# Values one head later and scores ahead of a sum in an attention, and experts chosen by one maximum and one replacement

## The chip, the core and the metric

The kernel runs on one core of a Trainium2 chip. A core has five engines that run their own instruction streams and meet only at semaphores: TensorE (PE in the profile, with its weight loads as PEld), VectorE (DVE), ScalarE (ACT), GpSimd (POOL) and SyncE (SP), which here only issues transfers. The metric is the device time of one execution, in microseconds (us); lower is better.

## The reference

The program is two transformer blocks on 256 tokens of width 1024, in float32. The first block has two mixers side by side: an eight-head causal attention with compressed queries and keys (MLA), and an RWKV-7 recurrence. Then comes a mixture of 32 experts, of which each token takes 4. The second "block" is two layers of dense FFN and mixers. What the change touches is the attention of the first block and the choice of experts:

```python
def one_block(args):                       # causal_attention, 8 heads, Q_BLOCK = 128
    qb, bi = args
    scores = jnp.einsum('bqhd,bkhd->bhqk', qb, k, preferred_element_type=jnp.float32) * scale
    ...
    probs = jax.nn.softmax(scores, axis=-1).astype(v.dtype)
    return jnp.einsum('bhqk,bkhd->bqhd', probs, v)

logits = (ht @ router_w + router_b).astype(jnp.float32)     # moe_ffn, 256 tokens x 32 experts
top_val, top_idx = lax.top_k(logits, TOP_K)                 # TOP_K = 4
gates = jax.nn.softmax(top_val, axis=-1)
...
counts = jnp.bincount(e_flat, length=N_EXPERTS)
```

In between, `mod = silu(c) @ ada_w + ada_b` gives six vectors that shift, scale and gate the blocks; the kernel computes them in three thirds.

## The kernel before

The program is a row of stages, each a block of five streams written by hand, with a barrier at its end; nothing reorders instructions inside a stream. `Steps.step` lets an engine signal a semaphore and wait for it itself; `Steps.tell` only signals. Tensors lie transposed, channels on the 128 partitions and tokens along the row.

Weights of 1 MB each come through `ring` (12 slots of 8 KB per partition), and later also `ring_odd`. SP issues a load as soon as the semaphore `used` says that TensorE has finished with what was in the slot.

The **attention stage** (`c3`, from line 634 on). TensorE first makes the second third of `mod` (`sum_ada(pe, 1, ...)`), then queries and keys head by head, their rotated partners (`partner`, with DVE's `rotate`) and the values' inputs `v_nat`. Then `sum_ada(pe, 2, bank[5])` makes the last third: 32 products with 8 MB of weights. ACT copies the sum to `mod_rows`, TensorE turns it, DVE adds the bias. Only then `att_pe`, `att_dve` and `att_act` run, which `attention(n, scale)` has built. In them one head goes through:
- TensorE `scores(h)` into bank h % 2 (L522), two heads ahead;
- DVE `soften(h)`: mask (L558), row maximum (L560), its negative (L562);
- ACT `exps(h)`: exponential and its sum (L597);
- DVE `divide(h)`: reciprocal (L567) and scaling (L570);
- TensorE `turn(h)`: three 128x128 transposes (L530);
- ACT: the copy `turned` (L606);
- TensorE `values(h)`: two products (L538, L539); for each second head DVE's `take` copies the result (L575).

The **choice of experts** is the end of stage `c7` (from line 1395 on). After a layer norm ACT makes `hT` in eight pieces (L1486), TensorE multiplies each by the router's weights (L1452) into four groups, ACT copies `groups` (L1488), TensorE adds them (L1457), and DVE adds the bias: `logits`, 128 tokens x 2 tiles x 32 experts. Four rounds on DVE find the largest, mark the first place where it stands (`hit`, with the helper numbers `rev`), add the mark to `chosen` and lower it in `work`. `chosen_ready` lets TensorE count, with triangular and full matrices of ones in float32 (L1463 to L1467), each token's rank within its expert. DVE makes `rank`, and `passes`, the number of times that the loop over experts has to run (64 slots each). ACT meanwhile copies `h_nat`, scales `xT` for the residual (L1494, L1498) and makes the exponential of the shifted logits for the `gates` (L1496). Then the stage ends, each engine reads `passes`, and the expert stage begins (`pick`, L1783; gather; the products with the experts' weights, whose first loads into freed slots SP issues while the first expert is being computed).

## Time and profile before

| | |
|---|---|
| median of three runs | 2384.93 us |
| the three runs | 2393.33, 2380.46, 2384.93 us |
| the profiled execution | 2385.3 us |
| its span, first to last instruction | 2383.5 us |
| mean granted TensorE clock | 0.965 |
| busy: PE, PEld, DVE, ACT | 2204.9, 1595.3, 1098.5, 701.9 us |
| DMA | 626.63 MB, mean 263 GB/s |

### The profile page before, as it was taken

What the parts mean: (1) busy time and instruction counts of PE and PEld (TensorE: products, weight loads), DVE (VectorE), ACT (ScalarE), POOL (GpSimd) and SP (SyncE); (2) the same over time, 40 slices, a digit from 0 to 9 for tenths busy, and PEclk for the clock granted to TensorE, in tenths of its full rate; (3) what the DMA queues carried; (4) which work ended last, traced back from release to release, by engine and by line L of the source; (5) the groups of instructions that cost most, each with busy time, mean ns of one, the idle gap of its engine ahead of it and who ended that gap; (6) DMA issues with size and microseconds to landing.
All of it is one profiled execution on the core that took longest, in us unless ns stands there. A gap on an engine that the chain in (4) does not pass through costs nothing. (4 is left out here: it accounts for less than half of the span.)

```text
span 2383.5 us, 37791 instructions
## 1 busy us (share of the span) xinstructions
PE 2204.9 (93%) x15730; PEld 1595.3 (67%) x15730; DVE 1098.5 (46%) x1701; ACT 701.9 (29%) x889; POOL 16.9 (1%) x16
## 2 busy tenths in 40 slices
PE   6978869999999999999997999999999999999998
PEld 4637733443333333333336999989999999989997
DVE  4567331221111111111116666777556656677664
ACT  3353231111111111111114334545334334445332
POOL 0002000000000000000000000000000000000000
PEclk9988989999999999999998999999999999999999
DMA  9640279999999999999985655334565555433651
GB/s 390 257 175 3 98 299 424 424 425 425 425 425 425 425 426 425 426 425 425 414 351 170 202 186 173 119 105 136 195 194 171 184 188 166 142 106 125 208 180 53
DMA packets 233056, 626.63 MB, mean 263 GB/s; under 512 B 13144, under 2 KB 149880, under 8 KB 197112
## 3 DMA queue, kind: packets, MB, share of 16 engines
q1 hardware_dynamic: 229736, 622.06, 68.4%
q10 hardware_dynamic: 3216, 3.06, 0.4%
q8 instruction: 80, 1.31, 0.2%
q14 instruction: 24, 0.20, 0.0%
HBM read 624.03 MB, written 1.05 MB: 262 GB/s over the span
## 5 line engine op out<-in xcount | busy, mean ns | idle before, releaser
L1929 DVE TENSOR_TENSOR w_low<-ring,w_high 128x2048 fp32r<-128x2048 f32 x168 | 383.9, 2290 | 266.6 <-ACT w_high L1924 266.6
L1924 ACT ACTIVATE w_high<-ring 128x2048 fp32r<-128x2048 f32 x168 | 320.1, 1910 | 274.2 <-PE bank L2163 140.8
L1682 PE MATMUL bank<-ring,ut 128*64 128x512 f32 x1024 | 252.7, 646 | 43.2 <-DMA ring<-in_exp_w_dram 42.8
L1654 PE MATMUL bank<-ring_odd,xt 128*64 128x512 f32 x1024 | 225.0, 597 | 0.0
L1654 PE MATMUL bank<-ring,xt 128*64 128x512 f32 x1024 | 223.3, 594 | 0.3 <-ACT xt L1736 0.3
L1682 PEld LDWEIGHTS bank<-ring,ut 128*64 128x64 f32 x1024 | 74.2, 146 | 205.9 <-issue 134.5
L2178 PE MATMUL bank<-h_high,w_high 128*128 128x256 f32 x1408 | 187.4, 282 | 6.5 <-ACT h_high L2069 3.6
L2178 PE MATMUL bank<-h_high,w_low 128*128 128x256 f32 x1408 | 186.6, 281 | 1.4 <-DVE w_low L1929 1.4
L2178 PE MATMUL bank<-h_low,w_high 128*128 128x256 f32 x1408 | 186.5, 281 | 1.3 <-DVE h_low L2108 1.3
L2178 PEld LDWEIGHTS bank<-h_high,w_high 128*128 128x128 f32 x1408 | 176.0, 189 | 7.6 <-ACT h_high L2069 4.3
L1740 ACT ACTIVATE sg<-glu 128x512 f32<-128x512 f32 x32 | 20.2, 631 | 543.0 <-DVE glu L1803 543.0
L2178 PEld LDWEIGHTS bank<-h_high,w_low 128*128 128x128 f32 x1408 | 175.8, 189 | 1.7 <-DVE w_low L1929 1.7
L2178 PEld LDWEIGHTS bank<-h_low,w_high 128*128 128x128 f32 x1408 | 175.8, 189 | 1.5 <-DVE h_low L2108 1.5
L1819 DVE SCALAR_TENSOR_TENSOR xT<-bank,mod,xT 128x256 f32<-128x256 f32 x128 | 55.6, 480 | 247.4 <-PE bank L1696 247.4
L1654 PEld LDWEIGHTS bank<-ring_odd,xt 128*64 128x64 f32 x1024 | 72.5, 138 | 144.3 <-issue 144.3
L1654 PEld LDWEIGHTS bank<-ring,xt 128*64 128x64 f32 x1024 | 72.3, 137 | 143.2 <-issue 143.2
L1802 DVE TENSOR_SCALAR lin<-bank 128x256 f32<-128x256 f32 x64 | 26.7, 418 | 257.2 <-PE bank L1654 257.2
L1795 DVE TENSOR_SCALAR choose<-base 128x128 fp32r<-128x128 f32 x32 | 9.1, 287 | 244.0 <-PE bank L1682 244.0
L1753 ACT ACTIVATE y<-bank 64x512 f32<-64x512 f32 x64 | 37.9, 592 | 270.3 <-PE bank L1682 269.5
L2163 PE MATMUL bank<-u_low,w_high 128*128 128x256 f32 x704 | 92.0, 279 | 0.0
L2163 PE MATMUL bank<-u_high,w_high 128*128 128x256 f32 x704 | 91.9, 279 | 0.0
L2163 PE MATMUL bank<-u_high,w_low 128*128 128x256 f32 x704 | 91.9, 279 | 0.0
(542 smaller groups left out, 2834.1 us busy)
## 6 DMA issues: line engine op xcount, KB each, us to landing
ring<-in_exp_w_dram SPq DMA_DIRECT2D x256, 1024.0 KB, 22.0
ring_odd<-in_exp_w_dram SPq DMA_DIRECT2D x128, 1024.0 KB, 21.0
ring<-in_ffn_w_gate_dram SPq DMA_DIRECT2D x44, 1024.0 KB, 5.4
ring<-in_ffn_w_up_dram SPq DMA_DIRECT2D x44, 1024.0 KB, 5.4
ring<-in_ffn_w_down_dram SPq DMA_DIRECT2D x44, 1024.0 KB, 5.0
ring<-in_w_in_dram SPq DMA_DIRECT2D x36, 1024.0 KB, 5.4
ring<-in_ada_w_dram SPq DMA_DIRECT2D x24, 1024.0 KB, 12.5
ring<-in_w_out_dram SPq DMA_DIRECT2D x8, 1024.0 KB, 5.2
```

The lines of the kernel that those rows point to most:

```text
L1654: ins = nc.tensor.matmul(bank[b][at:at + SLOTS, :], xt[:, c, SLOTS * side:SLOTS * side + SLOTS], (ring, ring_odd)[side][:, c, 512 * q:512 ...
L1682: ins = nc.tensor.matmul(bank[2 + dh][64 * dh:64 * dh + 64, :], ut[:, r % 4, 64 * (r // 4):64 * (r // 4) + 64], w[:, x, 512 * dh:512 * dh ...
L1740: nc.scalar.activation(sg[:, :], glu[:, :], ACT.Sigmoid, scale=SW_ALPHA).then_inc(sem("sg_ready"), 1)
L1753: nc.scalar.activation(y[64 * side:64 * side + 64, 512 * dh:512 * dh + 512], bank[2 + dh][64 * dh:64 * dh + 64, :], ACT.Copy).then_inc(sem ...
L1795: nc.vector.tensor_scalar(choose[:, side, :], const("half_of"), const("expert_of")[:, bass.ds(e, 1)], None, ALU.mult).then_inc(sem("chosen ...
L1802: nc.vector.tensor_scalar(lin[:, 256 * b:256 * b + 256], pairs[:, :, 1], LIMIT, -LIMIT, ALU.min, ALU.max)
L1819: ins = nc.vector.scalar_tensor_tensor(xT[:, m, :], bank[6 + n % 2][:, T * j:T * j + T], mod[:, 40 + m:41 + m], xT[:, m, :], ALU.mult, ALU ...
L1924: nc.scalar.activation(w_bufs[0][u % BUFS], ring2[:, u % RING2, :], ACT.Copy).then_inc(high2, 1)
L1929: nc.vector.tensor_tensor(w_bufs[1][u % BUFS], ring2[:, u % RING2, :], w_bufs[0][u % BUFS].bitcast(F32), ALU.subtract).then_inc(low2, 1)
L2163: ins = nc.tensor.matmul(sums(m // 2)[:, T * (m % 2):T * (m % 2) + T], w[:, at:at + P], v[:, T * x:T * x + T], start=(g == 0 and k == 0 an ...
L2178: ins = nc.tensor.matmul(b[:, T * x:T * x + T], w[:, at:at + P], h[:, c, :], start=(k == 0 and x == 0 and c == 0), stop=(k == 2 and c == D ...
```

## The change

In the attention:
- `values(h - 1)` stands ahead of `turn(h)`, behind `scores(h + 2)`; the last `values` comes after the loop.
- The functions take callbacks. `queries_ready(h)` waits only for the rotation of head h's pair. `scores(0)` and `scores(1)` are issued first, then `before_turns` (`sum_ada(pe, 2, ...)`), and `after_second` turns the sum behind `turn(1)`. On ACT the copy of the sum comes behind `exps(1)`, on DVE the bias behind the first `take`.
- The second attention of the kernel, of another block, has its own code and is not touched.

In the choice of experts:
- `hT`: five pieces on ACT, three on DVE (`H_ON_ACT = 5`).
- `nc.vector.max` gives the eight largest logits of each token, one instruction for each tile of 128 tokens; the fifth to eighth are overwritten with `ABSENT` (-3.0e38); `match_replace` copies the logits and puts `TAKEN` (-3.3e38) where one of the remaining four values stands; `chosen` is where copy and logits differ. Four columns that hold `ABSENT` stand behind the 32 logits, to match the four overwritten values.
- `chosen`, `before_r` and `ones_r` are F32R, so each rank product is one MATMUL instead of two; ACT makes the two copies.
- Three comparisons for `passes` become one, against `limits`; the gates come last on DVE.

```diff
...
-            def tensor(pe, S, lhs, rhs, v):
+            def tensor(pe, S, lhs, rhs, v, queries_ready, before_turns, after_second):
...
                 def scores(h):
+                    queries_ready(h)
                     if h >= 2:
...
                 scores(1)
+                before_turns()
...
                         scores(h + 2)
+                    if h:
+                        values(h - 1)
                     turn(h)
-                    values(h)
-            def vector(dve, st, S, mask, dst):
+                    if h == 1:
+                        after_second()
+                values(n - 1)
+            def vector(dve, st, S, mask, dst, after_third):
...
                         take(h // 2 - 1)
+                    if h == 2:
+                        after_third()
                 take(n // 2 - 1)
-            def scalar(act, st, S):
+            def scalar(act, st, S, after_two):
...
                 exps(1)
+                after_two()
...
                 pe.wait_ge(sem("k_taken"), HEADS)
-                sum_ada(pe, 2, bank[5])
-                pe.wait_ge(sem("v_taken"), 1)
-                pe.wait_ge(sem("mod_rows_ready"), 2)
...
-                pe.wait_ge(sem("rotated"), PAIRS_Q)
                 pe.wait_ge(sem("k_spread"), 1)
+                def last_third():
+                    sum_ada(pe, 2, bank[5])
+                    pe.wait_ge(sem("partner_taken"), 1 + PAIRS_Q)
+                    pe.wait_ge(sem("v_taken"), TT)
+                def turn_last_third():
+                    pe.wait_ge(sem("mod_rows_ready"), 2)
+                    for k in range(4):
+                        ins = nc.tensor.transpose(bank[6][:, P * k:P * k + P], mod_rows[:, P * k:P * k + P], ident)
+                    ins.then_inc(sem("mod_turned"), 1)
                 att_pe(pe, S,
...
                        lambda h, keys: k_all[:, h, 0:keys],
-                       lambda h, a: v_nat[:, a, VDIM * h:VDIM * h + VDIM])
+                       lambda h, a: v_nat[:, a, VDIM * h:VDIM * h + VDIM],
+                       lambda h: pe.wait_ge(sem("rotated"), h // 2 + 1),
+                       last_third, turn_last_third)
...
                 nc.scalar.activation(ps[:, 13, :], ps[:, 13, :], ACT.Sigmoid)
-                act.wait_ge(used, UNIT[("ada2", ADA_THIRD - 1)] + 1)
-                act.wait_ge(sem("mod_turned"), 1)
-                st.tell(nc.scalar.activation(mod_rows[:, :], bank[5][:, :], ACT.Copy), "mod_rows_ready")
-                att_act(act, st, S)
+                def last_third():
+                    act.wait_ge(used, UNIT[("ada2", ADA_THIRD - 1)] + 1)
+                    act.wait_ge(sem("mod_turned"), 1)
+                    st.tell(nc.scalar.activation(mod_rows[:, :], bank[5][:, :], ACT.Copy), "mod_rows_ready")
+                att_act(act, st, S, last_third)
...
                 rotate(PAIRS_Q - 1)
-                dve.wait_ge(sem("mod_turned"), 2)
...
-                att_dve(dve, st, S, const("causal3"), lambda pair: hT[:, pair, :])
+                def last_third():
+                    dve.wait_ge(sem("mod_turned"), 2)
+                    dst, bias = mod_third(2)
+                    st.step(nc.vector.tensor_tensor(dst, turned_columns(bank[6][:, :]), bias, ALU.add), "mod_taken")
+                    st.step(nc.vector.tensor_scalar(mod[:, 32:48], mod[:, 32:48], 1.0, None, ALU.add))
+                att_dve(dve, st, S, const("causal3"), lambda pair: hT[:, pair, :], last_third)
...
+            logits = sb("logits", [P, TT, E + 8 - TOPK], where=c7)
...
+            chosen = sb("chosen", [P, TT, E], F32R, where=c7)
+            chosen_f = chosen[:, :, :].bitcast(F32)
+            top = sb("top", [P, TT, 8], where=c7)
...
+            before_r = sb("before_r", [P, P], F32R, where=c7)
+            ones_r = sb("ones_r", [P, P], F32R, where=c7)
...
                 for c in range(DC):
-                    pe.wait_ge(sem("h_ready"), c + 1)
+                    if c < H_ON_ACT:
+                        pe.wait_ge(sem("h_ready"), c + 1)
+                    else:
+                        pe.wait_ge(sem("h_ready_dve"), c - H_ON_ACT + 1)
                     j = c % 4
...
+                pe.wait_ge(sem("rank_parts"), 1)
                 pe.wait_ge(sem("chosen_ready"), 1)
-                nc.tensor.matmul(bank[5][:, 0:E], const("before"), chosen[:, 0, :], start=True, stop=True)
...
+                nc.tensor.matmul(bank[5][:, 0:E], before_r[:, :], chosen[:, 0, :], start=True, stop=True)
+                nc.tensor.matmul(bank[5][:, E:2 * E], before_r[:, :], chosen[:, 1, :], start=True, stop=False)
+                nc.tensor.matmul(bank[5][:, E:2 * E], ones_r[:, :], chosen[:, 0, :], start=False, stop=True)
...
+                nc.tensor.matmul(bank[5][:, 2 * E:3 * E], ones_r[:, :], chosen[:, 1, :], start=False, stop=True).then_inc(sem("ranks_ready"), 1)
...
                     nc.scalar.activation(xT[:, 4 * j:4 * j + 4, :], xT[:, 4 * j:4 * j + 4, :], ACT.Copy, scale=ALPHA).then_inc(sem("x_scaled"), 1)
+                nc.scalar.activation(before_r[:, :], const("before"), ACT.Copy)
+                nc.scalar.activation(ones_r[:, :], ones, ACT.Copy).then_inc(sem("rank_parts"), 1)
                 act.wait_ge(sem("b_loaded"), 128)
...
                 act.wait_ge(sem("h_gain_ready"), 1)
-                for c in range(DC):
+                for c in range(H_ON_ACT):
                     act.wait_ge(sem("scaled"), c // 2 + 1)
...
-                rev = const("rev").unsqueeze(1).to_broadcast([P, TT, E])
+                for c in range(H_ON_ACT, DC):
+                    dve.wait_ge(sem("scaled"), c // 2 + 1)
+                    st.tell(nc.vector.tensor_scalar(hT[:, c, :], xT[:, c, :], h_gain[:, 0, c:c + 1], h_gain[:, 1, c:c + 1],
+                                                    ALU.mult, ALU.add), "h_ready_dve")
+                for j in range(3):
+                    nc.vector.memset(limits[:, j:j + 1], SLOTS * (j + 1) + 0.5)
+                st.step(nc.vector.memset(logits[:, :, E:], ABSENT))
                 wide = lambda ap: ap.to_broadcast([P, TT, E])
+                scores = logits[:, :, 0:E]
                 dve.wait_ge(sem("logits_ready"), 1)
                 dve.wait_ge(sem("router_loaded"), 32)
-                st.step(nc.vector.tensor_tensor(logits[:, :, :], bank[7][:, 0:TT * E].rearrange("p (a e) -> p a e", a=TT),
+                st.step(nc.vector.tensor_tensor(scores, bank[7][:, 0:TT * E].rearrange("p (a e) -> p a e", a=TT),
                                                 b_r[:, :].unsqueeze(1).to_broadcast([P, TT, E]), ALU.add))
-                nc.vector.memset(chosen[:, :, :], 0.0)
-                st.step(nc.vector.tensor_copy(work[:, :, :], logits[:, :, :]))
-                for k in range(TOPK):
-                    st.step(nc.vector.tensor_reduce(top[:, :, k], work[:, :, :], AX_X, ALU.max))
...
-                st.step(nc.vector.tensor_tensor(work[:, :, :], logits[:, :, :], wide(top[:, :, 0:1]), ALU.subtract), "shifted_logits")
-                st.tell(nc.vector.tensor_copy(hit[:, 0, 0:1], top[:, 0, 0:1]), "chosen_ready")
-                dve.wait_ge(sem("exp_ready"), 1)
...
+                for a in range(TT):
+                    ins = nc.vector.max(top[:, a, :], logits[:, a, 0:E])
+                st.step(ins)
+                st.step(nc.vector.memset(top[:, :, TOPK:], ABSENT))
+                for a in range(TT):
+                    ins = nc.vector.match_replace(left[:, a, :], top[:, a, :], logits[:, a, :], TAKEN)
+                st.step(ins)
+                st.step(nc.vector.tensor_tensor(chosen[:, :, :], left[:, :, 0:E], scores, ALU.not_equal), "chosen_ready")
+                st.step(nc.vector.tensor_tensor(work[:, :, :], scores, wide(top[:, :, 0:1]), ALU.subtract), "shifted_logits")
                 dve.wait_ge(sem("ranks_ready"), 1)
-                st.step(nc.vector.scalar_tensor_tensor(rank[:, :, :], bank[5][:, 0:TT * E].rearrange("p (a e) -> p a e", a=TT), 1.0, chosen[:, :, :],
+                st.step(nc.vector.scalar_tensor_tensor(rank[:, :, :], bank[5][:, 0:TT * E].rearrange("p (a e) -> p a e", a=TT), 1.0, chosen_f,
                                                        ALU.add, ALU.mult))
                 st.step(nc.vector.tensor_scalar(rank[:, :, :], rank[:, :, :], 1.0, None, ALU.subtract))
                 st.step(nc.vector.tensor_reduce(most[:, 0:1], bank[5][:, 2 * E:3 * E], AX_X, ALU.max))
-                for j in range(1, 4):
-                    st.step(nc.vector.tensor_scalar(most[:, j:j + 1], most[:, 0:1], SLOTS * j + 0.5, None, ALU.is_gt))
+                st.step(nc.vector.tensor_tensor(most[:, 1:4], most[:, 0:1].to_broadcast([P, 3]), limits[:, :], ALU.is_gt))
                 st.step(nc.vector.tensor_reduce(most[:, 0:1], most[:, 1:4], AX_X, ALU.add))
                 st.step(nc.vector.tensor_scalar(passes[:, :], most[:, 0:1], 1.0, None, ALU.add))
+                dve.wait_ge(sem("exp_ready"), 1)
+                st.step(nc.vector.tensor_tensor(gates[:, :, :], work[:, :, :], chosen_f, ALU.mult))
+                st.step(nc.vector.tensor_reduce(total_gate[:, :], gates[:, :, :], AX_X, ALU.add))
+                st.step(nc.vector.reciprocal(total_gate[:, :], total_gate[:, :]))
+                nc.vector.tensor_tensor(gates[:, :, :], gates[:, :, :], wide(total_gate[:, :].unsqueeze(2)), ALU.mult)
         if stop == "mix_out":
...
```

TensorE, the end of the products before the attention and the attention's first two heads, of before (`ring,base` is the last `partner`, `ring,c_wide` the sum, `base,mod_rows` its turn, `ring` alone the scores, `base,probs` a turn, `turned,v_nat` the values):

```order
L673 MATMUL bank<-ring,base 32x512
L292 MATMUL bank<-ring,c_wide 32x512 x32
L712 MATMUL bank<-base,mod_rows 128x128 x4
L522 MATMUL bank<-ring 128x128
L522 MATMUL bank<-ring 128x256
L522 MATMUL bank<-ring 128x128
L522 MATMUL bank<-ring 128x256
L522 MATMUL bank<-ring 128x128
L522 MATMUL bank<-ring 128x256
L530 MATMUL bank<-base,probs 128x128 x3
L538 MATMUL bank<-turned,v_nat 64x256
```

And of the changed kernel:

```order
L685 MATMUL bank<-ring,base 32x512
L526 MATMUL bank<-ring 128x128
L526 MATMUL bank<-ring 128x256
L526 MATMUL bank<-ring 128x128
L526 MATMUL bank<-ring 128x256
L295 MATMUL bank<-ring,c_wide 32x512 x32
L526 MATMUL bank<-ring 128x128
L526 MATMUL bank<-ring 128x256
L534 MATMUL bank<-base,probs 128x128 x3
L526 MATMUL bank<-ring 128x128
L526 MATMUL bank<-ring 128x256
L542 MATMUL bank<-turned,v_nat 64x256
```

The scores of heads 0 and 1 now stand ahead of the 32 products of the sum, its turn is further behind, and the values of head 0 follow the scores of head 3 instead of the turn of head 0.

DVE, from the logits through the first of four rounds, of before (the rounds' seven instructions L1533 to L1539 follow three more times):

```order
L1528 TENSOR_TENSOR logits<-bank,b_r 128x64
L1530 MEMSET chosen 128x64
L1531 COPY work<-logits 128x64
L1533 TENSOR_REDUCE top<-work 128x2
L1534 TENSOR_TENSOR hit<-work,top 128x64
L1535 TENSOR_TENSOR hit<-hit,base 128x64
L1536 TENSOR_REDUCE top<-hit 128x2
L1537 TENSOR_TENSOR hit<-base,top 128x64
```

And of the changed kernel, from the logits to `chosen`:

```order
L1572 TENSOR_TENSOR logits<-bank,b_r 128x2x32
L1575 MAX top<-logits 128x8 x2
L1577 MEMSET top 128x2x4
L1579 MATCH_REPLACE left<-top,logits 128x36 x2
L1581 TENSOR_TENSOR chosen<-left,logits 128x64
```

Four rounds of seven instructions, a memset and a copy have become two maxima, a memset, two replacements, and the comparison of the next fence.

DVE from there to the end of the stage, of before:

```order
L1541 TENSOR_TENSOR work<-logits,top 128x64
L1542 COPY hit<-top 128x1
L1544 TENSOR_TENSOR gates<-work,chosen 128x64
L1545 TENSOR_REDUCE top<-gates 128x2
L1546 RECIPROCAL top<-top 128x2
L1547 TENSOR_TENSOR gates<-gates,top 128x64
L1550 SCALAR_TENSOR_TENSOR rank<-bank,chosen 128x64
L1552 TENSOR_SCALAR rank<-rank 128x64
L1554 TENSOR_REDUCE most<-bank 128x1
L1556 TENSOR_SCALAR most<-most 128x1 x3
L1557 TENSOR_REDUCE most<-most 128x1
L1558 TENSOR_SCALAR passes<-most 128x1
```

And of the changed kernel:

```order
L1583 TENSOR_TENSOR work<-logits,top 128x64
L1585 SCALAR_TENSOR_TENSOR rank<-bank,chosen 128x64
L1587 TENSOR_SCALAR rank<-rank 128x64
L1588 TENSOR_REDUCE most<-bank 128x1
L1589 TENSOR_TENSOR most<-most,limits 128x3
L1590 TENSOR_REDUCE most<-most 128x1
L1591 TENSOR_SCALAR passes<-most 128x1
L1593 TENSOR_TENSOR gates<-work,chosen 128x64
L1594 TENSOR_REDUCE total_gate<-gates 128x2
L1595 RECIPROCAL total_gate<-total_gate 128x2
L1596 TENSOR_TENSOR gates<-gates,total_gate 128x64
```

The signal for the ranks comes with the comparison; rank and passes now stand ahead of the gates, with three instructions fewer.

## Rows read from the trace of the kernel before

**Rows 1.** The head of the page, whole kernel.
```profile
span 2383.5 us, 37791 instructions
```
**Rows 2.** Windows: stretch, length, busy us of each engine, clock, DMA share, GB/s.
```profile
core 0: us, PE busy (x) PEld busy (x) DVE busy (x) ACT busy (x) POOL busy (x), PEclk, DMA share, GB/s
...
129.50:135.10 5.60, 2.86 (x16) 2.04 (x16) 3.59 (x14) 3.53 (x9) 0.00 (x0) 1.00 1.02 429
137.10:141.00 3.90, 3.32 (x11) 2.20 (x11) 1.95 (x7) 1.51 (x6) 0.00 (x0) 0.50 1.01 429
...
149.00:153.00 4.00, 2.84 (x16) 1.76 (x15) 3.55 (x14) 2.17 (x7) 0.00 (x0) 1.00 0.00 0
...
400.00:800.00 400.00, 378.26 (x1797) 154.75 (x1793) 79.18 (x214) 43.29 (x77) 0.00 (x0) 0.98 1.02 425
```
**Rows 3.** Timeline at the attention's start: start us, length us, engine, line, instruction.
```profile
122.42 7.07 PE L292 MATMUL bank<-ring,c_wide 128*32 128x512 f32 x64
...
124.56 0.68 DVE L794 TENSOR_TENSOR ring<-ring 32x512 f32<-32x512 f32 x1
129.56 0.60 ACT L754 ACTIVATE mod_rows<-bank 128x512 f32<-128x512 f32 x1 [5.13 <-PE bank L292]
...
135.11 0.55 PE L530 MATMUL bank<-base,probs 128*128 128x128 f32 x3 [1.89 <-DVE probs L570]
```
**Rows 4.** Timeline of one head in the attention's steady state.
```profile
147.77 0.92 PE L522 MATMUL bank<-ring 96*128 96x128 f32 x4
...
148.53 0.49 PE L530 MATMUL bank<-base,probs 128*128 128x128 f32 x3
148.73 0.56 DVE L558 TENSOR_TENSOR masked<-bank,base 128x384 f32<-128x384 f32 x1 [0.57 <-PE bank L522]
...
149.60 0.65 PE L538 MATMUL bank<-turned,v_nat 128*64 128x256 f32 x2 [0.58 <-ACT turned L606]
...
150.04 0.42 DVE L575 COPY hT<-bank 128x256 f32<-128x256 f32 x1
...
150.38 0.15 DVE L567 RECIPROCAL den<-den 128x2 f32<-128x2 f32 x1
150.39 0.92 PE L522 MATMUL bank<-ring 96*128 96x128 f32 x4
...
150.57 0.55 DVE L570 TENSOR_SCALAR probs<-probs,den 128x128 f32<-128x128 f32 x2
```
**Rows 5.** Timeline: two turns of slow heads, the last turn, the last copy.
```profile
138.58 0.85 PE L530 MATMUL bank<-base,probs 128*128 128x128 f32 x3
...
142.92 0.85 PE L530 MATMUL bank<-base,probs 128*128 128x128 f32 x3
...
155.39 0.55 PE L530 MATMUL bank<-base,probs 128*128 128x128 f32 x3
...
157.42 0.42 DVE L575 COPY hT<-bank 128x256 f32<-128x256 f32 x1 [2.85 <-PE bank L539]
```
**Rows 6.** Timeline of the choice of experts, to the expert stage's first pick.
```profile
309.52 4.04 ACT L1486 ACTIVATE hT<-xT,h_gain 128x256 f32<-128x256 f32 x8 [2.61 <-DVE xT L1383]
...
314.62 0.38 ACT L1488 ACTIVATE groups<-bank 128x256 f32<-128x256 f32 x1 [1.06 <-PE bank L1452]
...
315.72 0.23 DVE L1528 TENSOR_TENSOR logits<-bank,b_r 128x64 f32<-128x64 f32 x1 [4.50 <-PE bank L1457]
...
320.10 1.28 ACT L1496 ACT_TABLE_LOAD   x1
...
323.22 0.15 DVE L1542 COPY hit<-top 128x1 f32<-128x1 f32 x1
323.38 2.06 ACT L1498 ACTIVATE xT<-xT,x_gain 128x256 f32<-128x256 f32 x4
...
325.81 0.23 DVE L1550 SCALAR_TENSOR_TENSOR rank<-bank,chosen 128x64 f32<-128x64 f32 x1 [1.36 <-PE bank L1467]
...
327.27 0.15 DVE L1558 TENSOR_SCALAR passes<-most 128x1 int32<-128x1 f32 x1
329.25 0.74 DVE L1783 TENSOR_SCALAR pick<-base,rank 128x64 f32<-128x64 f32 x4 [1.82 <-PEq L222]
```

31 lines of the change are left out of this document (7 added, 24 removed).

## The prediction

> **What bounds the kernel now.** I read the page first: one core, a span of 2383.5 us [rows 1], far longer than either edited place, so the question is whether time won in the two places travels to the end. Then the windows, to see what each stretch is limited by [rows 2]. From 400 to 800 us the DMA engines move 425 GB/s with a share of 1.02: the expert stage is a stream of weights. That stream cannot begin early by itself, because the DMA queue waits until the first expert's matmuls release slots of the ring; what comes before it shifts it, as a whole. The edited places both lie before it, in stages that do not wait for bulk transfers: from 149 to 153 us, in the middle of the attention, nothing moves at all [rows 2]. So I take every microsecond won at the end of the attention, or at the end of the stage that chooses the experts, as one microsecond of the kernel. Next I read the timeline of the two places row by row: where the attention starts [rows 3], one head of its steady state [rows 4], a slow head and the tail [rows 5], and the choice of experts [rows 6].
>
> **The attention before.** `sum_ada(2)` holds TensorE from 122.42 for 7.07 us; ACT copies its rows at 129.56; only then come four turns, the scores, the softening on DVE, and the first probabilities are turned at 135.11 [rows 3]. In the steady state scores of one head start at 147.77 and of the next at 150.39: 2.62 us a head. In it TensorE spends 0.76 on scores (147.77 to 148.53), then turns at 148.53, and `values` of the same head cannot start before 149.60, with 0.58 us of idle time in front, ended by ACT's copy `turned`; values take 0.79 [rows 4]. That wait is TensorE's own and lies inside every head.
>
> **The attention after.** Three edits work here.
> (a) scores(0) and scores(1) go ahead of `sum_ada(2)`. They cost 2 x 0.76 = 1.5 us in front of it, so it ends at 122.42 + 1.5 + 7.07 = 131.0. Meanwhile DVE, free after its last rotation at 124.56 + 0.68 = 125.24 [rows 3], softens both (1.31 each, 148.73 to 150.04 in [rows 4]) by 127.9. ACT's exponentials follow at once, as in the steady state, where DVE's divide at 150.38 has not waited for them. So the softening, the exponentials and `divide(0)` cost nothing: what hides them is `sum_ada`, with about 2 us to spare; without that cover they would cost the 3.3 us that follow here as a gain. At 131.0 TensorE makes scores(2) and turns head 0 at 131.0 + 0.76 = 131.8, against 135.11: 3.3 us earlier. What is queued behind the moved sum: the copy of its rows on ACT (before `turned`, 0.6 us), four turns on TensorE behind turn(1), two small DVE instructions behind the first `take`. On the DMA queue, eight loads of 1 MB for expert 0 wait for the slots of this sum; they go out 1.5 us later and are not wanted before the expert stage, so nothing.
> (b) `values(h-1)` stands ahead of `turn(h)`. TensorE then has scores 0.76, values 0.79 and a turn of 0.53 in a row, 2.1 us a head, with no wait of its own. DVE becomes the bound: soften 1.31 + divide 150.38 to 150.57 + 0.55 = 0.74, every second head the copy `take`, 0.34 (150.04 to 150.38) [rows 4]. From 131.9, when scores(2) are there, DVE has six softens (7.9), seven divides (5.2), three takes (1.0) and the two moved instructions (0.4): 14.5 us, to 146.4.
> (c) The tail: turn(7) now stands behind values(6), so about 147.2 instead of 146.4; from turn(7) to the end of the last take it was 155.39 to 157.42 + 0.42 = 2.45 [rows 5] and stays so. The attention ends at 149.6, against 157.84: **8.2 us** earlier. What follows (squares, sums, root) is unchanged.
> About 2.6 of these 8.2 are no merit of the order in the code. Head to head at 138.58 and 142.92 is 4.34 us, not 2.62 [rows 5], with a granted clock of 0.50, the 1.2 GHz level, from 137.10 [rows 2]. From 135.11 over 138.58 to 142.92 that makes 3.47 + 4.34 - 2 x 2.62 = 2.6. Before the clock fell TensorE had been busy 2.86 of 5.60 us; from 149 to 153, at 2.4 GHz, 2.84 of 4.00 [rows 2]. The new order is denser than either (2.1 busy of 2.25), and comes straight from `sum_ada`. I take the full clock.
>
> The Trainium skill, "TensorE: Matmul & The Clock Gate", section "What's actually happening", says that the throttled level is the default and that activity lifts it; the section "A second HAM failure mode: psum-queue depth-cycling" says that many short idles between groups of matmuls that cycle through PSUM banks make the clock swing between its levels. By the first the new order keeps the clock; by the second it could lose it again. The trace here shows both levels in the same attention; the second is a rival below.
>
> **The choice of experts before.** Logits are added at 315.72; 28 small instructions in four rounds follow until `chosen_ready` at 323.22 + 0.15 = 323.37; five rank matmuls, rank at 325.81; `passes` is written at 327.27 + 0.15 = 327.42, the stage ends, and the first `pick` is at 329.25 [rows 6]. DVE is the chain; ACT loads its table at 320.10, is ready at 321.38, and waits for DVE.
>
> **After.** (d) hT: ACT makes 5 of 8 pieces. Eight take 4.04 from 309.52 [rows 6], 0.52 apart, so the fifth ends at 312.0. DVE stands idle for 4.50 us before 315.72, from 311.2 on, and makes the other three in at most 0.35 each (two such scalings of probabilities are 0.55 in [rows 4]): 312.3 against 313.56. The router matmuls follow with little delay: the copy `groups`, 314.62 before, comes **1.1 us** earlier (between 0, if TensorE turns out to be the limit, and 1.4).
> (e) 28 instructions become two MAX, a memset, two MATCH_REPLACE and a comparison. The trace has neither operation. The nearest rows are DVE's on 64 elements, 32 of which, from 315.72 to 323.22, start 0.23 apart; I take 0.25 for each of the four, and allow from 0.1 to 1.0. With 0.30 for logits, 0.15 for the memset and 0.26 for the comparison it is 1.7 us: chosen at 315.72 - 1.1 + 1.7 = 316.3. The rank matmuls with one-pass operands I leave at the old 2.6 (323.22 to 325.81) as the upper bound, half of it as the lower: rank by 318.9. From rank to `passes` it was 1.6; two instructions fewer make 1.25: 320.2 at the latest.
> (f) So DVE is no longer the end. ACT is late next: its table is ready at 321.38 - 1.1 = 320.3, the exponential 0.2 later, then four more scalings of xT, 2.06 [rows 6]: **322.5**. DVE's gates come behind the exponential and need 0.95: 321.4, with 1.1 to spare. The stage ends at 322.5 instead of 327.42: **4.9 us** earlier. Two small extra copies on ACT (for the one-pass operands) stand where ACT waited for the biases, and the memsets of DVE where it waits for the logits: nothing. If the four unknown instructions cost 1.0 each, chosen is 3.0 later; 1.1 to 1.3 of that is hidden, and 3.1 remain of the 4.9.
>
> **Sum.** 8.2 + 4.9 = 13.1 us. The profiled execution took 2385.3 us, 1.8 more than its span and 0.4 more than the median: 2385.3 - 13.1 = 2372.2. I forecast 2372, 0.54% below the median. The first gather then stands on the same idle TensorE as before, so I leave its clock as it is.
>
> **Rivals.**
> 1. The clock falls in the new attention as well, the rule above. At 1.2 GHz a head is bound by TensorE at about 4.34 - 0.58 = 3.8 instead of 2.25; a stretch as long as the old one holds two heads, 3 us: saving 10, 2375. If it lasted all through, 12 us: the attention would end 4 later than before, saving 1, 2384. For it: the swing in the old trace with gaps of only 2 us. Against it: from 149 to 153 it stayed at 2.4 GHz with more idle time. Chance 0.22, nearly all of it for the short form.
> 2. It does not do what it says in the experts' choice: the router matmuls are bound by TensorE and the new instructions at 1.0 each, so 2 us instead of 4.9; 2375. Chance 0.12.
> 3. Given back later: low-clock stretches of the following stages fall elsewhere, or the stream of weights runs a little slower; three runs of the old kernel lie 13 us apart. Saving 3 to 8: 2380. Chance 0.13.
> 4. Slower: MAX and MATCH_REPLACE as one costly mechanism. They stand between the logits and the rank matmuls, so in all what goes over 1.2 us of extra cost shows. It decides from 13.1 + 1.2 = 14.3 us, or 3.6 us for each of the four; at 6.6 each, 2397. Against it: the short DVE rows here cost 0.15 to 0.25, whatever the operation. Chance 0.02.
>
> **Numbers.** The forecast's own case, savings of 11 to 16, has 0.51. About 0.5%, 11.9 us, is what a measurement of this kernel tells from no change, and the forecast lies just beyond it: of its own case four fifths are beyond (0.41), of rival 1 a fifth (0.05), and luck with the clock in the later stages adds 0.05: faster 0.51, within 0.46, slower 0.03 (rival 4 and what I have not thought of). The range takes in rivals 1 and 2 and part of 3 above, and below the upper bounds of (d), (e) and a clock that stays up later: 2364 to 2380.
>
> **What would show it.** Right: the first turn of probabilities at about 131.8; turns 2.2 to 2.3 us apart with DVE hardly idle; clock 1.00 through the heads; the last take near 149.6; `chosen` 1.5 to 2 us behind the logits; the last instruction of the choosing stage on ACT, with DVE done before it; first `pick` 13 us earlier. Wrong: a wait of DVE or TensorE for ACT inside a head; the stage's end still on DVE; the expert stream at less than 425 GB/s.

## The result and the profile after

The changed kernel takes 2378.02 us, median of 20 runs (2371.15 to 2380.88); the kernel before, in 20 runs beside it, 2389.56 us (2380.46 to 2404.76). The ratio is 0.9945, 95% interval 0.9931 to 0.9959, or 13.1 us of 2389.56 (9.8 to 16.5); the means lie 13.1 us apart, the medians 11.5. The forecast was a saving of 13.1 us and a time of 2372, with a range of 2364 to 2380. The time lies 6 us above 2372, mostly since the three runs of before that the forecast started from have a median of 2384.93, and the 20 have one 4.6 us higher.

The head of the page of the changed kernel, which answers to [rows 1]:

```profile
span 2374.9 us, 37769 instructions
```

This pair of profiled executions is only 8.6 us apart. What stands ahead of the attention is the same program in both, but the attention begins at 122.42 us before and at 126.44 after. So I read each place from its own start. TensorE's timeline of the attention in the changed kernel (start us, length us, engine, line, instruction, idle time before it and what ended it), which answers to [rows 3] to [rows 5]:

```profile
126.44 1.58 PE L526 MATMUL bank<-ring 96*128 96x128 f32 x8
127.94 7.07 PE L295 MATMUL bank<-ring,c_wide 128*32 128x512 f32 x64
134.95 0.92 PE L526 MATMUL bank<-ring 96*128 96x128 f32 x4
135.71 0.49 PE L534 MATMUL bank<-base,probs 128*128 128x128 f32 x3
...
142.71 0.55 PE L534 MATMUL bank<-base,probs 128*128 128x128 f32 x3 [0.32 <-DVE probs L579]
143.09 0.82 PE L526 MATMUL bank<-ring 96*128 96x128 f32 x4
143.84 0.65 PE L542 MATMUL bank<-turned,v_nat 128*64 128x256 f32 x2
...
144.67 0.55 PE L534 MATMUL bank<-base,probs 128*128 128x128 f32 x3
...
150.86 0.55 PE L534 MATMUL bank<-base,probs 128*128 128x128 f32 x3
...
154.46 3.68 PE L742 MATMUL bank<-sq,base 128*128 128x256 f32 x8 [1.61 <-ACT sq L779]
...
162.94 1.31 PE L893 MATMUL bank<-ps,w_kv 64*128 64x256 f32 x5 [3.09 <-PEq L225]
```

DVE's last `take` there:

```profile
152.89 0.42 DVE L584 COPY hT<-bank 128x256 f32<-128x256 f32 x1 [2.81 <-PE bank L543]
```

The reader is to see four things. The scores of two heads stand ahead of the sum, and the first turn comes 9.27 us after the start, against 12.69. Values follow scores with no wait for `turned`, and the wait that is left in front of a turn is for DVE's `probs`; only the values of the last three heads, with no scores ahead of them, still wait 0.58 us for `turned`. The last turn is 15.15 us behind the first, against 20.28. And the squares behind the attention take 3.68 us, where before they took 1.99:

```profile
158.99 1.99 PE L723 MATMUL bank<-sq,base 128*128 128x256 f32 x8 [1.61 <-ACT sq L757]
```

Windows of the changed kernel (stretch, length, busy us of PE, PEld, DVE, ACT, POOL, clock, DMA share, GB/s) tell why:

```profile
135.00:140.00 5.00, 4.63 (x31) 3.39 (x29) 3.88 (x15) 3.25 (x10) 0.00 (x0) 1.00 1.00 418
140.00:145.00 5.00, 4.68 (x29) 3.01 (x28) 4.72 (x18) 3.14 (x12) 0.00 (x0) 1.00 1.01 428
...
155.00:157.00 2.00, 2.00 (x6) 1.65 (x5) 0.00 (x0) 1.74 (x2) 0.00 (x0) 0.50 0.00 0
```

The clock stays up through the heads and falls behind them. The choice of experts in the changed kernel, which answers to [rows 6]:

```profile
306.68 2.57 ACT L1522 ACTIVATE hT<-xT,h_gain 128x256 f32<-128x256 f32 x5 [2.61 <-DVE xT L1408]
...
308.30 1.05 DVE L1562 TENSOR_SCALAR hT<-xT,h_gain 128x256 f32<-128x256 f32 x3
...
310.76 0.39 ACT L1524 ACTIVATE groups<-bank 128x256 f32<-128x256 f32 x1 [1.51 <-PE bank L1485]
...
312.21 0.23 DVE L1572 TENSOR_TENSOR logits<-bank,b_r 128x64 f32<-128x64 f32 x1 [2.81 <-issue]
312.47 0.29 DVE L1575 MAX8 top<-logits 128x8 f32<-128x32 f32 x2
...
312.92 0.09 DVE L1579 MATCH_VALUE_LOAD left<-top,logits 128x8 f32 x1
313.00 0.18 DVE L1579 MATCH_REPLACE8 left<-top,logits 128x36 f32<-128x36 f32 x1
...
313.38 0.23 DVE L1581 TENSOR_TENSOR chosen<-left,logits 128x64 fp32r<-128x64 f32 x1
...
314.56 0.23 DVE L1585 SCALAR_TENSOR_TENSOR rank<-bank,chosen 128x64 f32<-128x64 f32 x1 [0.70 <-PE bank L1501]
...
315.66 0.15 DVE L1591 TENSOR_SCALAR passes<-most 128x1 int32<-128x1 f32 x1
316.52 1.28 ACT L1532 ACT_TABLE_LOAD   x1
317.81 0.26 ACT L1532 ACTIVATE work<-work 128x64 f32<-128x64 f32 x1
317.98 2.06 ACT L1534 ACTIVATE xT<-xT,x_gain 128x256 f32<-128x256 f32 x4
318.17 0.23 DVE L1593 TENSOR_TENSOR gates<-work,chosen 128x64 f32<-128x64 f32 x1 [2.36 <-ACT work L1532]
...
321.94 0.74 DVE L1821 TENSOR_SCALAR pick<-base,rank 128x64 f32<-128x64 f32 x4 [2.83 <-PEq L225]
```

The last instruction of the stage is now ACT's xT, which ends at 320.04, 13.36 us behind the start of hT's scaling; before, the end was on DVE, at 17.90. DVE now stands still for 2.36 us before its gates, which end 0.93 us ahead of ACT. The two traces side by side, all in us:

| stretch | before | after | difference |
|---|---|---|---|
| span's start to the attention's first scores or sum | 122.42 | 126.44 | +4.02 |
| from there to the end of the last `take` | 35.42 | 26.87 | -8.55 |
| from there to the next stage's first matmul | 8.23 | 9.63 | +1.40 |
| from there to hT's scaling | 143.45 | 143.74 | +0.29 |
| hT's scaling to the first `pick` | 19.73 | 15.26 | -4.47 |
| first `pick` to the span's end | 2054.25 | 2052.96 | -1.29 |

### The profile page after: what moved, and what is told of

The parts are those of the page before. It is cut to its first block and busy times, and to the rows that moved or that the text cites. A ratio compares the mean times of both kernels' runs of the same rounds, so it can differ in the third digit from the quotient of the medians.

```text
span 2374.9 us, 37769 instructions
## 1 busy us (share of the span) xinstructions
PE 2199.2 (93%) x15725; PEld 1595.6 (67%) x15725; DVE 1093.6 (46%) x1683; ACT 700.5 (29%) x888; POOL 16.9 (1%) x16
## 3 DMA queue, kind: packets, MB, share of 16 engines
q10 hardware_dynamic: 3216, 3.06, 0.4%
```

## The experiments

**The attention alone and the choice of experts alone.** Each is the kernel before with one part of the change's diff and nothing of the other.

The runs `lag_only`, `early_only`, `ht_on_act`, `ranks_two_pass`, `choose_x8`, `act_relieved` and `act_relieved_table`, which come further below, were executed once each and are read from their traces alone.

> The kernel before with the whole attention part of the change and nothing of the choice of experts. The length of the attention is read from its first instruction on TensorE (sum or scores) to the end of the last `take`: 35.42 us before, 26.87 in the changed kernel. My theory (the attention part is worth its forecast 8.2 us by itself, and passes 1:1): length 26.9 to 27.5, turns 2.3 apart, whole kernel 8 to 9 us (0.35%) below the kernel before, ratio near 0.9965. Rival, the old low-clock stretch was most of the gain: then the clock falls to 0.50 in here again and the length is 29.5 or more, and the kernel gains 5 to 6 us. Rival, given back later: length 27, but the whole kernel within 3 us of before.

> The kernel before with the change to the choice of experts alone. Read from the start of hT's scaling to the first `pick`: 19.73 us before, 15.26 in the changed kernel. My theory (the part is worth about 4.5 us whatever the attention does): 15.2 to 15.5 here, whole kernel 4 to 5 us below before, ratio near 0.998; the two parts alone add up to the whole change. Rival, the parts overlap or one is given back: the whole kernel less than 2 us below before though the stretch is 15.3.

Measured, attention alone: ratio 0.9961 (0.9939 to 0.9983), 9.3 us, between 4.1 and 14.6; the attention from 125.62 to 152.49, 26.87 long. Experts alone: ratio 0.9968 (0.9947 to 0.9989), 7.7 us, between 2.6 and 12.7; from 318.90 to the pick at 334.15, 15.25. The product of the two, 0.9929, agrees with 0.9945 within the intervals, which are some us wide and could hide a loss of that size. The traces are finer: each stretch has alone the length that it has in the changed kernel, 26.87 and 15.25 for 26.87 and 15.26. So the parts add, and neither eats the other.

The second of these traces told more than it was made for. Its attention has the old order and begins 9.5 us later than in the kernel before. TensorE's timeline there:

```profile
131.92 7.07 PE L295 MATMUL bank<-ring,c_wide 128*32 128x512 f32 x64
...
144.62 0.55 PE L533 MATMUL bank<-base,probs 128*128 128x128 f32 x3 [1.89 <-DVE probs L573]
...
148.17 0.85 PE L533 MATMUL bank<-base,probs 128*128 128x128 f32 x3
...
152.51 0.79 PE L533 MATMUL bank<-base,probs 128*128 128x128 f32 x3
```

and a window of it; in the next microsecond the clock is 0.50:

```profile
146.00:147.00 1.00, 1.00 (x5) 0.58 (x4) 0.53 (x2) 0.90 (x4) 0.00 (x0) 0.64 1.05 442
```

The slow head of 4.34 us is there again (148.17 to 152.51), and the clock falls between 146 and 147, 14 to 15 us behind the sum's start; in the kernel before it is 0.93 from 136 to 137 and 0.50 from 137 to 138, 14 to 15 us behind too. Both executions with the old order have the fall at the same place; the twelve others, below, have none there.

**Each half of the attention part alone.** `lag_only`, whole:

```diff
                     if h + 2 < n:
                         scores(h + 2)
+                    if h:
+                        values(h - 1)
                     turn(h)
-                    values(h)
+                values(n - 1)
```

`early_only`, its core (the sum is in `before_turns`, the turn of its rows in `after_second`; the moves on ACT and DVE are those of the change):

```diff
                 for h in range(n):
...
                     turn(h)
+                    if h == 1:
+                        after_second()
                     values(h)
...
-                sum_ada(pe, 2, bank[5])
...
+                def last_third():
+                    sum_ada(pe, 2, bank[5])
```

> The kernel before with values(h-1) put ahead of turn(h) and nothing else. My theory (DVE becomes the bound at 2.25 to 2.35 us a head instead of 2.62): eight turns 2.3 apart where the clock is at its upper level, TensorE's wait of 0.58 for `turned` in front of values gone or moved to a wait for DVE in front of turns; the attention 35.42 - 7 x 0.3 = 33.2 with the old low-clock stretch, 30.6 without it. Rival, the softening waits for scores, which now start later behind values, so DVE is not full and the pitch stays above 2.5.

> The kernel before with the first two scores ahead of the sum, and the sum's followers moved, but values of a head still behind its own turn. My theory: from the first scores to the first turn 9.3 us instead of 12.69 (122.42 to 135.11), pitch 2.6 as before; length 35.42 - 3.3 = 32.1 with a low-clock stretch in the heads, 29.5 without. This also tells whether the low clock came from the idle time of 3 us before the first turn: by my theory that the dense stretch in front keeps the clock, it stays at 1.00. Rival: the clock falls where a period of its own puts it, whatever the order, and here again in the heads.

Measured for `lag_only`: the attention from 125.45 to 154.97, 29.52 long; the clock 1.00 in every head. Its timeline:

```profile
125.45 7.07 PE L292 MATMUL bank<-ring,c_wide 128*32 128x512 f32 x64
...
138.14 0.55 PE L530 MATMUL bank<-base,probs 128*128 128x128 f32 x3 [1.88 <-DVE probs L572]
...
140.11 0.55 PE L530 MATMUL bank<-base,probs 128*128 128x128 f32 x3
...
142.07 0.55 PE L530 MATMUL bank<-base,probs 128*128 128x128 f32 x3
...
144.37 0.55 PE L530 MATMUL bank<-base,probs 128*128 128x128 f32 x3 [0.30 <-DVE probs L572]
...
156.12 1.99 PE L725 MATMUL bank<-sq,base 128*128 128x256 f32 x8 [1.60 <-ACT sq L759]
```

Two pitches are to be seen: 1.97 us where DVE has no `take` between the turns, 2.30 where it has one. For `early_only` the first turn is 9.27 us behind the first scores (122.41):

```profile
131.68 0.49 PE L534 MATMUL bank<-base,probs 128*128 128x128 f32 x3
```

The heads are 2.62 to 2.68 apart, but for one of 3.07, in which DVE adds the sum's bias, and the length is 29.57, to 151.98. Its clock is 1.00 through the heads too, and lower only behind them (windows):

```profile
140.00:150.00 10.00, 7.38 (x39) 4.53 (x39) 7.09 (x26) 4.92 (x16) 0.00 (x0) 1.00 0.65 273
153.00:156.00 3.00, 2.87 (x9) 2.35 (x10) 0.04 (x1) 2.41 (x3) 0.00 (x0) 0.65 0.00 0
```

What the slow stretch cost the old attention is to be read over three heads: its first turns are 3.47, 4.34 and 2.98 us apart, and at the upper clock three heads take 3 x 2.63, so it cost 2.9. The prediction's 2.6 left out the third head, whose turn is slow too. Without it the old attention would be 35.42 - 2.9 = 32.5 long. So the early scores give 2.9, the lagged values 3.0, both 5.6; and either alone gives the 2.9 of the clock as well. Together they give 0.3 less than one by one: behind the early scores the first three heads are 2.31, 2.37 and 2.32 apart, in `lag_only` 1.97, 1.96 and 2.30, since DVE stood still until scores(2) and the sum's rows are turned between heads. That is 0.8 in all, of which `early_only` alone has 0.4 (its head of 3.07).

What was expected of `early_only` held at the value without a low-clock stretch. The lag is worth more than the 2.2 of its expectation (35.42 - 33.2), since heads without a `take` are 1.97 apart, not 2.3. That the fall comes at a time of its own, whatever the order, is hard to hold for these kernels: two executions with the old order, starting 9.5 us apart, had it at the same head, and none of twelve with either edit had it in a head. What keeps the clock up stays open. It is not the idle time before the first turn, which is the same in `lag_only` (1.88 us) as in the kernel before (1.89); nor is it denser heads, as those of `early_only` (TensorE busy 7.38 of 10.00 us in the window above) are about as dense as the old ones from 149 to 153 (2.84 of 4.00).

**Four probes of the choosing stage**, each one edit to the changed kernel.

`ht_on_act`:

```diff
-H_ON_ACT = 5
+H_ON_ACT = 8
```

`ranks_two_pass` (and the same for `before_r` and `ones_r`):

```diff
-            chosen = sb("chosen", [P, TT, E], F32R, where=c7)
+            chosen = sb("chosen", [P, TT, E], where=c7)
```

`choose_x8`, in place of the block done once:

```diff
+                for _ in range(8):
+                    for a in range(TT):
+                        ins = nc.vector.max(top[:, a, :], logits[:, a, 0:E])
+                    st.step(ins)
+                    st.step(nc.vector.memset(top[:, :, TOPK:], ABSENT))
+                    for a in range(TT):
+                        ins = nc.vector.match_replace(left[:, a, :], top[:, a, :], logits[:, a, :], TAKEN)
+                    st.step(ins)
```

`late_stream`, behind the gates:

```diff
+                for _ in range(4):
+                    st.step(nc.vector.reciprocal(total[:, :], root[:, :]))
+                    st.step(nc.vector.reciprocal(groups[:, :], root[:, :]))
```

> The changed kernel with all eight scalings of hT on ACT again (H_ON_ACT = 8). Read from the start of hT's scaling: to the copy `groups` 4.08 us in the changed kernel, 5.10 in the one before. My theory (the split is worth 1.0 us and all of it reaches the stage's end, since ACT is late there and does the scalings too): groups at 5.1, logits 1.0 later, the last instruction of the stage on ACT at 14.4 instead of 13.36, the first `pick` at 16.3 instead of 15.26. Rival, the router's matmuls set the pace (the split was for nothing): groups below 4.5. Second rival, the delay is swallowed by ACT's later idle time: groups at 5.1 and pick still at 15.3.

Measured: groups 5.19 behind hT's start, chosen 0.82 later than in the changed kernel, the stage's end on ACT at 14.19 against 13.36. The split is worth 0.8 at the stage's end, not swallowed. The pick moved by only 0.49 (15.75); the wait between the stages was 0.3 shorter in this execution. The expectation had 1.0 for all of it. Against the kernel before, `groups` comes 1.02 earlier but logits only 0.67 (5.53 behind hT's start for 6.20): four transposes of hT stand between on TensorE, and in the changed kernel they start while its clock is still 0.50 (310 to 311 us) and take 0.91 us, 310.65 to 311.56, where before they took 0.54, 314.51 to 315.05.

> The changed kernel with float32 operands for the five rank matmuls again, instead of the one-pass type. In the changed kernel they start 0.11 us apart and `rank` comes 1.2 us behind `chosen`. My theory (they were most of the 1.4 us by which chosen-to-rank fell, and the saving hides behind ACT): rank some 2.2 to 2.6 us behind chosen as in the kernel before, passes 1.1 to 1.4 us later, stage end still on ACT and unmoved at 13.36 after hT's start, pick at 15.3. Rival, DVE and ACT are closer than the profile says: the stage's end moves by more than 0.3 us.

Measured: rank 1.76 behind chosen instead of 1.18, passes later by as much, the stage's end at 13.30 and the pick at 15.21, unmoved. The saving hides, as expected, but the two-pass form costs only 0.6, not 1.4. Its matmuls:

```profile
313.83 0.37 PE L1497 MATMUL bank<-chosen,before_r 128*128 128x32 f32 x2
314.03 0.39 PE L1498 MATMUL bank<-chosen,before_r 128*128 128x32 f32 x2
...
315.20 0.22 DVE L1585 SCALAR_TENSOR_TENSOR rank<-bank,chosen 128x64 f32<-128x64 f32 x1 [1.27 <-PE bank L1501]
```

They start 0.22 apart at a clock of 1.00. In the kernel before the same five were 0.43 apart. A window of the kernel before:

```profile
323.30:325.80 2.50, 2.34 (x10) 2.21 (x10) 0.91 (x5) 2.13 (x5) 0.00 (x0) 0.50 0.23 92
```

TensorE had then waited 5.93 us for `chosen`. So of the 1.41 won between chosen and rank, 0.58 are the one pass and 0.83 the clock: the earlier decision finds TensorE still at its upper level. `choose_x8`, next, shows the other way: with the decision late again the same one-pass matmuls follow 6.21 us of waiting and run at 0.50.

> The changed kernel with the block of two MAX, the memset and two MATCH_REPLACE done eight times over on the same operands; it computes the same. One block takes 0.9 us (312.47 to 313.38). My theory (DVE has slack, and ACT is the end of the stage): seven blocks more put chosen and shifted_logits 6.4 us later, to 320.2 on the clock of the changed kernel; ACT's exponential, at 317.81 now, is then the first thing that is late, by 2.4, and the stage ends 2.3 to 2.7 us later, at about 15.9 after hT's start, pick at 17.9: some 4 of 6.4 us hidden. Rival, no cover, as the forecast's price for the unknown instructions had it only down to 1.2 us: pick 5 us or more later. Second rival: the instructions pipeline when repeated and a block costs much less than 0.9.

Measured: one block 0.91 (logits to chosen 7.56 us, instead of 1.17), so repeated blocks do not overlap. ACT's exponential waits, 2.3 later than in the changed kernel. But the stage ends on DVE:

```profile
315.94 0.26 ACT L1532 ACTIVATE work<-work 128x64 f32<-128x64 f32 x1 [2.47 <-DVE work L1584]
...
317.12 0.23 DVE L1586 SCALAR_TENSOR_TENSOR rank<-bank,chosen 128x64 f32<-128x64 f32 x1 [1.21 <-PE bank L1501]
...
319.12 0.23 DVE L1597 TENSOR_TENSOR gates<-gates,total_gate 128x64 f32<-128x64 f32 x1
```

Counted from hT's scaling (302.50 here) the end is at 16.85, 3.5 later than without the repeats, and the pick at 18.76. Of 6.4 us 2.9 are hidden. My expectation named ACT and had 2.5: it forgot that ranks, passes and gates come behind `chosen` on DVE. They took 3.9, with the rank matmuls 0.21 apart at a clock of 0.50.

> The changed kernel with eight extra reciprocals of 128x256 on DVE (1.75 us each by the same instruction of the layer norm, 14 us together) at the very end of the choosing stage; their outputs are read by nobody. It measures the forecast's first step by itself, that every microsecond ahead of the expert stream is one of the kernel. My theory: the stage's end moves by 14 less the 1 us that DVE has to spare, 13 us, and the whole kernel is 13 us slower than the changed one, so about +1 to +5 us beside the kernel before (ratio near 1.000 where the changed kernel has 0.9945). Rival, the stream of weights absorbs part of it (transfers already under way, slots filled ahead): the whole kernel less than 7 us above the changed one, ratio 0.9975 or less.

Measured: hT's scaling to pick 28.98, which is 13.7 more; pick to the end of the span 2053.85 against 2052.96, nothing given back. The trace's pick:

```profile
336.85 0.75 DVE L1824 TENSOR_SCALAR pick<-base,rank 128x64 f32<-128x64 f32 x4 [2.16 <-PEq L225]
```

The ratio is 0.9984 (0.9966 to 1.0002); against 0.9945 that is 9.3 us, between about 4 and 15, so the times hold both 13.7 and the rival's 7, and the trace decides. Over the fourteen executions the stretch from pick to end took 2052.50 to 2057.76 us, so a pair shows this to a few us only; a stream that took in half of the 13.7 is excluded. Within that, what comes ahead of the stream passes through one to one.

**Who ends the stage.** `act_relieved` on the changed kernel (ACT, then DVE ahead of the gates; `X_ON_ACT` is 4). Besides taking four scalings from ACT it puts the exponential ahead of the others, so that DVE's gates need not wait:

```diff
-                for c in range(4):
-                    nc.scalar.activation(xT[:, c, :], xT[:, c, :], ACT.Identity, bias=x_gain[:, 1, c:c + 1], scale=x_gain[:, 0, c:c + 1])
                 act.wait_ge(sem("shifted_logits"), 1)
                 nc.scalar.activation(work[:, :, :], work[:, :, :], ACT.Exp).then_inc(sem("exp_ready"), 1)
-                for c in range(4, DC):
+                for c in range(X_ON_ACT):
...
+                for c in range(X_ON_ACT, DC):
+                    nc.vector.tensor_scalar(xT[:, c, :], xT[:, c, :], x_gain[:, 0, c:c + 1], x_gain[:, 1, c:c + 1], ALU.mult, ALU.add)
                 dve.wait_ge(sem("exp_ready"), 1)
```

`act_relieved_table` has `X_ON_ACT = 5`, the three other scalings on DVE (two behind `work`, one behind `passes`), and an early exponential of one element:

```diff
                 ln_act(act)
+                nc.scalar.activation(early[0:1, 0:1], early[0:1, 0:1], ACT.Exp)
                 act.wait_ge(sem("h_gain_ready"), 1)
```

> The changed kernel, with the exponential on ACT straight behind the h_nat copies, ahead of all xT scalings, and the last four of these eight scalings moved to DVE, ahead of its gates. It tests that ACT is what ends the stage in the changed kernel: there ACT does 8 scalings (4.12 us) and a table load (1.28) behind h_nat, and DVE stands still for 2.36 us before its gates. My theory: ACT ends 11.3 us behind the start of hT's scaling instead of 13.36, DVE (passes at 9.1, four scalings of 0.35, gates 1.0) at 11.5, the first `pick` at 13.4 instead of 15.26. Rival, a stage costs what its last dependency costs whoever does the scalings: pick still at 15 or later.

> As act_relieved, with three of the eight scalings on DVE, two of them where DVE waits for the ranks, and with an exponential of one element on ACT ahead of hT's scaling, so that the table is loaded while ACT waits for the layer norm. My theory: the load of 1.28 us leaves the path, ACT ends at 7.8 + 0.3 + 5 x 0.52 = 10.6 behind the start of hT's scaling, DVE at 10.5, pick at 12.5. Rival, the table is loaded again at the exponential, as the scalings in between take it away: then ACT ends near 11.9 and pick is at 13.8.

Measured: ACT ends at 11.40 and DVE at 11.38 behind hT's scaling, the pick is at 12.98, 2.3 earlier than in the changed kernel. With the early table:

```profile
305.07 2.57 ACT L1526 ACTIVATE hT<-xT,h_gain 128x256 f32<-128x256 f32 x5 [1.10 <-DVE xT L1409]
...
312.34 0.60 ACT L1531 ACTIVATE h_nat<-bank 128x512 f32<-128x512 f32 x1 [0.24 <-PE bank L1477]
312.83 0.25 ACT L1534 ACTIVATE work<-work 128x64 f32<-128x64 f32 x1
312.98 2.55 ACT L1536 ACTIVATE xT<-xT,x_gain 128x256 f32<-128x256 f32 x5
```

No load stands before the exponential, ACT ends at 10.46, DVE at 10.39, and the pick is at 12.37. The load now stands at 302.48, where ACT waits for the layer norm. ACT, with the exponential that DVE's gates wait for, was what ended the stage of the changed kernel.

**The copies of the attention on ACT**, with the same choosing stage, and the changed kernel beside it.

```diff
+                def take(pair):
+                    act.wait_ge(sem("out_ready"), 2 * pair + 2)
+                    st.tell(nc.scalar.activation(dst(pair), bank[4 + pair % 2][:, 0:T], ACT.Copy), "out_taken")
```

> As act_relieved_table, and in the attention the four `take` copies on ACT instead of DVE. DVE is the bound there with a mean pitch of 2.27 us a head (eight turns from 135.71 to 150.86 are 2.16 apart on the mean, the last two without softening). Without the copies DVE has 2.05 a head, TensorE 2.1. My theory: pitch of the turns 2.1 to 2.15 in the steady state, the attention 26.87 - 6 x 0.17 = 25.9 long, pick at 12.5 behind hT's start; together 3.7 us less than the changed kernel, a ratio to before of 0.9930 against 0.9945, too little for the times to tell, so it stands on the trace. Rival, the copies delay ACT's exponentials, which are in the loop too: pitch unchanged or longer.

> The changed kernel once more, beside take_on_act on one chip. By my theory the attention is 26.9 us long with the clock at 1.00 through the heads, wherever in the run it begins, as in both profiled runs with the old order the clock fell 14.7 us behind the sum's start. Ratio 0.9945 again. Rival, the clock's fall comes by its own phase: a second execution may have it in the heads, and the length is 29 or more.

Measured, `take_on_act`: turns 1.96 to 1.98 apart from 141.65 to 149.52, so DVE's copy was the 0.33 by which every second head was longer. The expectation's 2.1 for TensorE was too high, as the turns come closer than that. The attention is 26.15 long against 26.87, the pick at 12.73 (12.37 in `act_relieved_table`, with the same choosing stage); together 3.3 us less than the changed kernel. The ratio is 0.9917 (0.9886 to 0.9948), the changed kernel's beside it 0.9929 (0.9904 to 0.9954): it beats the kernel before, but the times don't tell it from the changed one. `after_again` has an attention of 26.85 us from 125.16, at a clock of 1.00 in its heads.

## Why the prediction was right

- **One to one.** Right, as finely as can be seen. From the pick to the end it is 2054.25 before and 2052.96 after, and the 13.7 us put in by `late_stream` came out as 13.7 at the pick and 14.6 at the end. From 400 to 800 us both kernels move 425 GB/s.
- **(a) Early scores, 3.3.** Right: the first turn 9.27 us behind the start for a forecast of 9.4, so 3.4 earlier; at the attention's end 2.9 of it are left when the edit stands alone, 2.7 when the lag is there too. DVE had done both softenings and waited 3.25 us for scores(2): the cover was ample.
- **(b) Lagged values.** The mechanism was right for the heads with scores left: DVE bounds them, and the wait for `turned` is gone. Mis-sized was DVE's need: 1.97 and 2.30 by turns, a mean of 2.13, for 2.25. The divide was counted as 0.74 to its last end, but the next softening starts 0.66 behind its start (137.22 to 137.88). TensorE's own need was put at 2.1; in `take_on_act` the turns are 1.96 apart. A wait of TensorE for ACT inside a head was named as a sign of being wrong. It is there in front of the values of the last three heads, 0.58 us each, since no scores stand between. The last turn came 24.42 us behind the start all the same, for a forecast of 24.8.
- **(c) The attention's end.** 26.87 us behind its start for 27.2; 8.55 saved for 8.2. The clock's part, 2.9 for 2.6 (the third head was left out), was rightly put down to the old order: the fall came back in the one other kernel that has that order, and in none with either edit. The reason given, a denser order, is not shown: `early_only` has heads as thin as the old ones and kept the clock. That the clock stayed up for the reason forecast can't be said; in that the term had luck.
- **Rival 1, the clock.** It did not come where it was forecast: no head slowed. But the clock fell behind the heads, at the squares, in every kernel with the early scores (3.06 to 3.68 us instead of 1.99), and the stretch to the next stage is 1.40 longer. "What follows (squares, sums, root) is unchanged" is the step of (c) that failed, and it cost 1.4 of 13: of the 2.9 that the clock gave in the heads, half is paid behind them. The Trainium skill, "TensorE: Matmul & The Clock Gate", section "A second HAM failure mode: psum-queue depth-cycling", says that frequent short idles between groups of matmuls that cycle through PSUM banks make the clock swing between its levels. The trace agrees only in part: the old order fell to 0.50 for two heads, but its later heads, with the same wait of 0.58 us in each, ran at 1.00, and so did all heads of the new order, with waits of 0.30 to 0.58.
- **(d) hT split, 1.1.** Mis-sized. The copy `groups` is 1.02 earlier, but logits only 0.67, and ACT's table for the exponential is loaded 11.1 us behind hT's start instead of 11.86, 0.7 earlier, where the forecast took off 1.1. By `ht_on_act` the split is worth 0.8.
- **(e) New instructions.** 1.40 us from the start of logits to the end of chosen for 1.7; the rank matmuls, left at the old 2.6, were 1.18 to rank. Neither changed the sum, since ACT ends the stage. That cover was said to be 1.1 to 1.3; `choose_x8` measured 2.9, since rank came 1.2 us behind chosen (1.7 in that run) and not 2.6, and ACT's end 0.4 later than forecast. Rival 4, slower by costly instructions, is far off: its point was 3.6 us each, and a MAX costs 0.15, a replacement with its value load 0.18.
- **(f) ACT is late next, 4.9.** Right: stage end 13.36 behind hT's start for a forecast of 12.98, the pick 4.47 earlier. The 0.4 is what (d) fell short. Shown by relieving ACT, which moved the end by 2 to 3 us.

Net, 8.55 + 4.47 - 1.40 = 11.6 us in the two places, against 13.1 forecast and 13.1 (9.8 to 16.5) timed. That the forecast and the timed saving are the same number is luck: the interval is 6.7 us wide, the medians give 11.5, and the traces' 11.6 is the forecast with 0.3 more in the attention, 0.4 less in the choosing stage and 1.4 less behind the attention. What the prediction got right is the mechanism of both parts and their sizes to half a microsecond.

## What to carry to other kernels

Read a small change from the start of its own stage: over fourteen profiled executions the attention began between 122.41 and 131.92 us behind an identical program, 9.5 us, most of what the whole change is worth. When a decision chain is made short, look at once for the engine that was merely in time before, here ACT with a table load and eight scalings; moving those gave another 2.9 us of stage for a few lines. And a term for a clock that stays up in one place needs its partner: ask where it will fall instead.

## What had not been expected of the hardware

- The time at which the same program reaches the attention goes with how long the clock was low ahead of it. From 0 to 120 us the mean granted clock was 0.96 in the two executions that got there first (122.41 and 122.42) and 0.87 in the last (131.92), with the eleven others between (0.90 to 0.94; it is 0.91 at 128.02 and 0.90 at 127.70, so the order is not strict). From 30 to 40 us and from 100 to 110 us it was 0.84 and 1.00 in the profiled run of before (start at 122.42), and in that of the experts alone (start at 131.92):

```profile
30.00:40.00 10.00, 6.13 (x26) 1.70 (x22) 1.51 (x5) 2.06 (x4) 0.00 (x0) 0.50 1.03 369
...
100.00:110.00 10.00, 10.00 (x47) 3.02 (x50) 7.68 (x12) 2.66 (x5) 0.00 (x0) 0.56 0.58 188
```

- Choosing the largest of 32 values per row is cheap: two maxima over 128x32 in 0.29 us, a replacement over 128x36 in 0.18 and 0.09 ahead of it to load its values. The whole block, with a memset between, repeats every 0.91 us in `choose_x8`, where the old four rounds took 6.7 (316.22 to 322.96).
- Five 128x128 by 128x32 matmuls start 0.11 us apart in one pass at a clock of 1.00 (changed kernel), 0.21 in one pass at 0.50 (`choose_x8`), 0.22 in two passes at 1.00 (`ranks_two_pass`) and 0.43 in two at 0.50 (kernel before).
